# A hybrid attention and delta-rule block on one core: wider products in the pair loop, with halves joined by VectorE, and four smaller moves

## The chip, the cores and the metric

The kernel runs on one core of a Trainium2 chip. The metric is the device time of one execution in microseconds; the times given are those of three executions, and one further execution was profiled. A core has five engines that run side by side and meet at semaphores: TensorE (PE, with its weight loads as PEld), VectorE (DVE), ScalarE (ACT), GpSimd (POOL) and SyncE (SP, which here only starts transfers). Each works through its own instructions in order, so an instruction that waits holds up all that is written behind it on the same engine.

## What is computed

One layer of an encoder block on x (256 rows, 2048 channels), all in 32-bit floats:

```
proj = x @ w_in + b_in                    # columns: aq ak av | dq dk dv dz | db da | ga gb
o_att = sliding-window attention with rotary positions and sinks (aq, ak, av)
q, k, v = silu(causal conv of width 4 (dq, dk, dv)); q, k L2-normalised per head
beta = sigmoid(db); g = -exp(a_log) * softplus(da + dt_bias)
o_dn = gated delta rule over 16 heads of 128, in chunks of 64:
       (I + A) u = beta v, A strictly lower triangular, then a scan over chunks
o_dn = rmsnorm(o_dn) * gain * silu(dz)
mix  = (sigmoid(ga) * (o_att @ w_br_att) + sigmoid(gb) * (o_dn @ w_br_dn)) @ w_out
h    = layernorm(alpha * x + mix)
out  = layernorm(alpha * h + swiglu(h) + sigmoid(h @ w_ple_gate + b) * (p @ w_ple_proj))
```

## The kernel before

**Products in two parts.** A product of 32-bit floats is made of three products of rounded numbers. ScalarE writes `hi`, the rounded copy of a weight tile (L1058), VectorE writes `lo = raw - hi` (L1402), and x lies as `xh` and `xl` in the same way. Both engines' helper is `split`. A quarter is one 128x512 piece of weights; `raw` holds four units of four quarters, loaded on SP's queue, and `hi` and `lo` are rings of eight quarters. The splits run six quarters (`LEAD`) ahead of TensorE, and ScalarE's split number n waits until TensorE has finished with quarter n - 8.

**Two kinds of quarters.** In most stages the weights stream: `rows_quarter` (L586 to L588) makes six products of 512 columns a quarter, with x as the stationary operand. In the pair loop the results are wanted with channels on the partitions, and `cols_quarter` (L574 to L576) has the weights stationary and streams x in 256 columns: for each of two tiles `kk` and two halves `f`, the three products hi\*xh, hi\*xl, lo\*xh go to the same 256 columns of `dense`, twelve products a quarter.

**The pair loop.** The delta rule is done in eight pairs of heads. `mixer_turn(i)` makes the products of pair i in 32 quarters, k = 0 to 31, eight each for dq, dk, dv, dz (s = 0 to 3); turn 0 is unrolled and turns 1 to 7 are a loop. The groups alternate between two pairs of banks of `dense`. ScalarE evicts a group with its bias into `pad` (`pad_in`, at k = 9, 17, 25) or, for dz, into `zb` (`chain_k`, stage 0, in the next turn), and VectorE makes the convolution from `pad`, one tap of one half at each k from 9 on (`conv`). Beside it every turn does one head group of the attention (`att_stage`, `att_k`).

**The chain.** While turn i makes pair i's products, all engines also work on the delta rule of pair i-1, which is one long chain of small steps. Every engine's program goes through the same numbers k, and at k it does the stage `stage_at(k)` of the chain behind its split. That is the whole order of the work: it is written out by hand. Before, `stage_at` gives k for k < 4, nothing at 4, the level matrix 0 (`FIRST`) at 5, and k - 2 from 6 on. The stages which the change and the prediction touch:

- stage 0: TensorE's `kk_qk` (L701, L708) writes k k^T and k q^T into the banks 0 and 1 of `C` (in the trace: chain). It waits for `silk` and `silq` (k and q after silu), and for `am`, the mask addition that VectorE made at k = 29 (L1592). ScalarE evicts `zb` and makes two tanh, for v and for the gate z; VectorE multiplies both (L1650).
- stages 1 to 3: `k_to_rows` (L714), ScalarE's squares (L1159), VectorE's row factors, the product `QKT` (L1656) and `AT` (L1668); ScalarE packs the diagonal blocks of `AT` into `VU` (L1175, L1177).
- the seed: GpSimd sets `VU[2]` to the unit matrix, multiplies the diagonal of `VU[0]` away and subtracts the unit matrix (L520 to L524).
- `FIRST` and stages 5, 7, 9, 11, 13: the inverse of I + A by doubling. VectorE transposes (L1620) and masks (L1622) into `Ym`, TensorE multiplies (`inv_level`, L740), ScalarE evicts (L1214). Level n's product stands at k = 7 + 2n. Stage 4 is an inverse root, eleven small VectorE operations.
- stages 15 to 17: the last doublings, `inv_last_y` (L749) and `inv_last_x` (L758).
- stages 18 to 22: the scan over chunks. L795 and L796 of stage 22 are its last products; ScalarE sums squares (L1203), VectorE adds (L1709).
- stage 23: a second inverse root, and the scaling `tmp` (L1713). Stage 26: transposes (`o_to_cols`, L802). Stage 27: VectorE multiplies with the gate into `odn` (L1717) and raises `on`.

The semaphore `on` is waited for by ScalarE at k = 31. The last pair's chain runs in the gate stage behind the loop, its stages spread over 54 of 64 quarters (`LAST_AT`).

**The start.** x comes in four parts (`x_part`) and is transposed on TensorE with `ident` (L615). The first weights come on ScalarE's queue in two pieces. `keep_busy` (L624) issues filler products before and after the first transposes; `WARM` says how many.

Of the kernel before, what the change touches and what calls it, by code (L numbers as in the profile page):

```python
# [18 lines left out]
F32 = mybir.dt.float32  # L19
F32R = mybir.dt.float32r  # L20
# [6 lines left out]
P = 128  # L27
# [16 lines left out]
WARM = (7, 7)  # L44
# [57 lines left out]
def stage_at(k):  # L102

    return k if k < 4 else k - 2 if k >= 6 else FIRST if k == 5 else None
# [18 lines left out]
def constants():  # L123
# [14 lines left out]
    c[:, C_OFF:C_OFF + 32] = i % 32 != j[:, 0:32]  # L138
# [30 lines left out]
def build(nc, A, out):  # L169
    ctx = ExitStack()  # L170
    with ctx:
# [23 lines left out]
        xh = place("xh", [P, KT, T], F32R)  # L195
        xl = place("xl", [P, KT, T], F32R)
# [157 lines left out]

        def flat2(m):
            return m.rearrange("p a b -> p (a b)")
# [30 lines left out]

        @block.sync
        def _(sp):
# [17 lines left out]

            x_part(0)
            sp.dma_start(ident[:], A["consts"][:, C_IDENT:C_IDENT + P]).then_inc(sem("ident_in"), 16)
# [67 lines left out]
        def _(pool):  # L477
# [38 lines left out]
            def inverse_seed(p):  # L516


                pool.wait_ge(sem("packed"), p + 1)
                pool.tensor_copy(VU[:, 2], four_of(cst[:, C_UNIT:C_UNIT + 32])).then_inc(sem("seed"), 1)  # L520
                pool.tensor_tensor(VU[:, 0], VU[:, 0], four_of(cst[:, C_OFF:C_OFF + 32]),
                                   ALU.mult).then_inc(sem("seed"), 1)
                pool.wait_ge(sem("seed"), 3 * p + 2)
                pool.tensor_tensor(VU[:, 0], VU[:, 0], four_of(cst[:, C_UNIT:C_UNIT + 32]),  # L524
                                   ALU.subtract).then_inc(sem("seed"), 1)

            decay_in(0)
            for p in range(PAIRS):
                inverse_seed(p)
# [33 lines left out]
        def _(pe):  # L563
            def cols_quarter(pos, n, j, bank, mh, ml):
# [3 lines left out]
                for kk in range(2):  # L568
                    k = 2 * j + kk
                    for f in range(2):  # L570
                        wh = hi[:, s, kk * 256 + f * P:kk * 256 + f * P + P]
                        wl = lo[:, s, kk * 256 + f * P:kk * 256 + f * P + P]
                        o = dense[:, bank + f, 0:T]
                        pe.matmul(o, wh, mh[:, k, :], start=(k == 0), stop=False)  # L574
                        pe.matmul(o, wh, ml[:, k, :], start=False, stop=False)  # L575
                        mm = pe.matmul(o, wl, mh[:, k, :], start=False, stop=(k == KT - 1))  # L576
# [120 lines left out]
            def kk_qk(p):  # L697
                pe.wait_ge(sem("silk"), p + 1)
                for x in range(4):
# [31 lines left out]
            def inv_level(p, n):  # L731


                pe.wait_ge(sem("y_out"), nth("y_out", n, p))
                if n:
# [147 lines left out]
            def mixer_turn(i, chain):  # L883

                pos = Pos(4 * U_LOOP, 32, i)
                for k in range(32):
                    s = k // 8
                    if k % 8 == 0:
                        if s == 0 and chain:
                            pe.wait_ge(sem("pad2"), i)  # L890
                        elif s == 1:
                            pe.wait_ge(sem("z_in"), i) if chain else pe.wait_ge(sem("rows_out"), 5)
# [1180 lines left out]
```

## Time and profile before

| | us |
|---|---|
| three executions, median (lowest to highest) | 1932.47 (1932.06 to 1932.5) |
| the profiled execution, its own time | 1932.79 |
| its span in the trace | 1931.0 |
| TensorE busy | 1914.2 |
| VectorE busy | 1269.9 |
| ScalarE busy | 1026.0 |
| GpSimd busy | 37.6 |

The span is the time from the first to the last instruction in the trace; the time of the execution holds 1.8 us around it. Busy time is the time covered by the records of an engine. TensorE's records overlap, since a matmul is recorded until its last result is out, so a stretch in which TensorE is busy throughout may still be one in which it is slower than it could be. In the timeline rows the columns are the start in us from the beginning of the span, the duration in us, the engine, the line and the operation, the output and the inputs, the shape, and the number of instructions merged into the row; in brackets stand the idle time ahead of it and what ended it.

### The profile page before, as it was taken

The page shows a single profiled execution, that of the slowest core. Times are in us where ns is not written, and L with a number is a line of the kernel's source. Part 1 is how long each engine was busy: PE and PEld are TensorE (multiplying, and loading weights), DVE is VectorE, ACT ScalarE, POOL GpSimd, SP SyncE. Part 2 cuts the span into 40 slices and gives each one's busy share as a digit, 9 for nine tenths or more (in the row PEclk, how much of TensorE's full clock was granted, in tenths as well). Part 3 has the DMA queues.
Part 4 walks back from the last instruction along what each step waited for, and adds up shares of the span by engine and source line. Part 5 has one row for each costly group of instructions (what it writes and reads, how often), then busy time and mean ns, then how long its engine had stood idle before and what let it go on. Part 6 is the DMA issues. An engine that isn't in the chain of part 4 may idle for free.

```text
span 1931.0 us, 29904 instructions
## 1 busy us (share of the span) xinstructions
PE 1914.2 (99%) x10563; PEld 1664.6 (86%) x10563; DVE 1269.9 (66%) x2349; ACT 1026.0 (53%) x2068; POOL 37.6 (2%) x79
## 2 busy tenths in 40 slices
PE   9999999999999999999999999999999999999997
PEld 8889999999999888888888788888888888888886
DVE  6657888888888756565665786555555555555555
ACT  4446666666666555455444554545444444444443
POOL 1000000000000000000000000000000000000000
PEclk9999999999999999999999999999999999999999
DMA  8665555455545557566566456555565555666552
GB/s 319 202 159 189 130 143 127 138 119 145 126 137 126 187 170 244 195 202 202 188 236 208 152 198 197 194 193 182 190 196 184 187 194 182 226 201 196 196 194 90
DMA packets 204180, 349.65 MB, mean 181 GB/s; under 512 B 6768, under 2 KB 73024, under 8 KB 203088
## 3 DMA queue, kind: packets, MB, share of 16 engines
q1 hardware_dynamic: 200560, 333.74, 52.6%
q0 software_dynamic: 3264, 14.47, 5.2%
q8 instruction: 44, 0.72, 0.1%
q10 hardware_dynamic: 288, 0.52, 0.1%
q14 instruction: 24, 0.20, 0.0%
HBM read 344.32 MB, written 2.10 MB: 179 GB/s over the span
## 4 chain that ended last, share of the span: by engine, by line
PE 94%; DVE 3%; ACT 1%; issue 1%; DMA 0%; DVEq 0%; SPq 0%; ACTq 0%
PE dense L586 23%; PE dense L588 23%; PE dense L587 23%; PE dense L574 5%; PE dense L575 5%; PE dense L576 5%; PE chain L740 2%; DVE lo L1402 1%; PE chain L822 1%; ACT sE L1238 1%; PE chain L1007 0%; ACT hi L1058 0%; PE chain L749 0%; PE chain L840 0%; PE chain L708 0%
## 5 line engine op out<-in xcount | busy, mean ns | idle before, releaser
L1402 DVE TENSOR_TENSOR lo<-raw,hi 128x512 fp32r<-128x512 f32 x1252 | 849.4, 690 | 525.4 <-ACT hi L1058 522.8
L1058 ACT ACTIVATE hi<-raw 128x512 fp32r<-128x512 f32 x1252 | 774.5, 630 | 628.1 <-PE dense L588 599.0
L586 PE MATMUL dense<-hi,xh 128*128 128x512 f32 x1376 | 539.9, 392 | 1.5 <-DVE xl L1949 1.1
L588 PE MATMUL dense<-lo,xh 128*128 128x512 f32 x1376 | 535.9, 389 | 0.0
L587 PE MATMUL dense<-hi,xl 128*128 128x512 f32 x1376 | 535.5, 389 | 0.0
L586 PEld LDWEIGHTS dense<-hi,xh 128*128 128x128 f32 x1376 | 258.5, 188 | 55.0 <-DVE xl L1949 2.0
L588 PEld LDWEIGHTS dense<-lo,xh 128*128 128x128 f32 x1376 | 258.3, 188 | 54.2
L587 PEld LDWEIGHTS dense<-hi,xl 128*128 128x128 f32 x1376 | 258.6, 188 | 52.4
L574 PE MATMUL dense<-xh,hi 128*128 128x256 f32 x1024 | 303.3, 296 | 0.0
L576 PE MATMUL dense<-xh,lo 128*128 128x256 f32 x1024 | 289.4, 283 | 0.0
L575 PE MATMUL dense<-xl,hi 128*128 128x256 f32 x1024 | 289.2, 282 | 0.0
L574 PEld LDWEIGHTS dense<-xh,hi 128*128 128x128 f32 x1024 | 195.6, 191 | 3.5 <-DVE lo L1402 3.1
L575 PEld LDWEIGHTS dense<-xl,hi 128*128 128x128 f32 x1024 | 195.9, 191 | 0.4
L576 PEld LDWEIGHTS dense<-xh,lo 128*128 128x128 f32 x1024 | 195.4, 191 | 0.0
L586 PE MATMUL dense<-hi,hh 128*128 128x512 f32 x328 | 127.7, 389 | 0.0
L588 PE MATMUL dense<-lo,hh 128*128 128x512 f32 x328 | 127.6, 389 | 0.0
L587 PE MATMUL dense<-hi,hl 128*128 128x512 f32 x328 | 127.6, 389 | 0.0
L586 PE MATMUL dense<-hi,bh 128*128 128x512 f32 x256 | 99.9, 390 | 0.0
L588 PE MATMUL dense<-lo,bh 128*128 128x512 f32 x256 | 99.6, 389 | 0.0
L587 PE MATMUL dense<-hi,bl 128*128 128x512 f32 x256 | 99.6, 389 | 0.0
L588 PEld LDWEIGHTS dense<-lo,hh 128*128 128x128 f32 x328 | 61.6, 188 | 12.9
L587 PEld LDWEIGHTS dense<-hi,hl 128*128 128x128 f32 x328 | 61.6, 188 | 12.8
(318 smaller groups left out, 1531.3 us busy)
## 6 DMA issues: line engine op xcount, KB each, us to landing
raw<-in_w_in_dram SPq DMA_DIRECT2D x115, 1024.0 KB, 5.1
raw<-in_w_ffn_gate_dram SPq DMA_DIRECT2D x44, 1024.0 KB, 5.1
raw<-in_w_ffn_up_dram SPq DMA_DIRECT2D x44, 1024.0 KB, 5.0
raw<-in_w_ffn_down_dram SPq DMA_DIRECT2D x44, 1024.0 KB, 5.0
raw<-in_w_br_att_dram SPq DMA_DIRECT2D x16, 1024.0 KB, 5.0
raw<-in_w_br_dn_dram SPq DMA_DIRECT2D x16, 1024.0 KB, 5.0
raw<-in_w_out_dram SPq DMA_DIRECT2D x16, 1024.0 KB, 5.0
raw<-in_w_ple_gate_dram SPq DMA_DIRECT2D x16, 1024.0 KB, 5.0
```

The lines of the kernel that those rows point to most:

```text
L574: pe.matmul(o, wh, mh[:, k, :], start=(k == 0), stop=False)
L575: pe.matmul(o, wh, ml[:, k, :], start=False, stop=False)
L576: mm = pe.matmul(o, wl, mh[:, k, :], start=False, stop=(k == KT - 1))
L586: pe.matmul(o, ah, hi[:, s, :], start=(k == 0), stop=False)
L587: pe.matmul(o, al, hi[:, s, :], start=False, stop=False)
L588: mm = pe.matmul(o, ah, lo[:, s, :], start=False, stop=(k == nk - 1))
L740: mm = pe.matmul(vu[:, :, x, :], Ym[:, x, :], VU[:, :, x, :], start=True, stop=True)
L822: mm = pe.matmul(o, qT[:, n, 2 * j:2 * j + 2, :].rearrange("p a c -> p (a c)"), kS[:, :, CH * n:CH * n + P], start=True, stop=True)
L1058: act.activation(parts(pos, n)[0], raw[:, slot, off:off + 512], ACT.Copy).then_inc(sem("hi_ready"), 1)
L1238: a = act.activation(m[:, r, :], m[:, r, :], ACT.Exp, bias=sm[:, 2, q:q + 1], scale=ATT_SCALE, accum_out=sm[:, 4, q:q + 1])
L1402: dve.tensor_tensor(wl, raw[:, slot, off:off + 512], wh.bitcast(F32), ALU.subtract).then_inc(sem("lo_ready"), 1)
```

## The change

Five things are done.

1. In `cols_quarter` the products hi\*xh and hi\*xl become one of 512 columns. `xh` and `xl` now lie side by side in one tile `xs`, so that one read gives both. The right half of a bank then holds hi\*xl, and the left one hi\*xh plus lo\*xh. ScalarE evicts the left half as before; VectorE adds the right one, into `pad` at the head of each convolution and into `zb` at stage 4. TensorE waits for these additions (`joined`) before it uses a pair of banks again.
2. The gate's tanh goes from stage 0 to stage 6 and its product from stage 0 to stage 8; the last wait for it is at the squares of the scan.
3. The diagonal is set by one minimum on VectorE at `FIRST`, instead of a multiplication and a subtraction on GpSimd, which keeps the copy of the unit matrix.
4. Stages from 16 on come one quarter later: `stage_at` gives k - 2 up to k = 17, nothing at 18 and k - 3 from 19 on. With that, `kk_qk` waits for `on` of the pair before, since both use bank 1 of `C`.
5. `ident` is the first transfer on SP's queue, the second piece of weights goes from ScalarE's queue to SP's behind the first part of x, and there are 12 and 5 fillers instead of 7 and 7.

The writes of `xh` and `xl` in the other stages (`x_hi`, `x_lo`, `merged_hi`, `merged_lo`, `h1_rows`) are only adapted to the layout and left out here.

```diff
 X_PARTS = (slice(0, 256), slice(256, 512), slice(512, 1024), slice(1024, 2048))
-WARM = (7, 7)
+WARM = (12, 5)
 LAST_AT = {1 + c * 54 // 30: c for c in range(31)}
...
-    return k if k < 4 else k - 2 if k >= 6 else FIRST if k == 5 else None
+    return k if k < 4 else k - 3 if k >= 19 else k - 2 if 6 <= k < 18 else FIRST if k == 5 else None
...
             c[:, C_LAST:C_LAST + 64] = m[:, 0:64]
-    c[:, C_OFF:C_OFF + 32] = i % 32 != j[:, 0:32]
+    c[:, C_OFF:C_OFF + 32] = np.where(i % 32 == j[:, 0:32], -1.0, np.finfo(np.float32).max)
     c[:, C_UNIT:C_UNIT + 32] = i % 32 == j[:, 0:32]
...
         x_at = at[0]
-        xh = place("xh", [P, KT, T], F32R)
-        xl = place("xl", [P, KT, T], F32R)
+        xs = place("xs", [P, KT, 2, T], F32R)
+        xh, xl = xs[:, :, 0, :], xs[:, :, 1, :]
         epsc = place("epsc", [P, 8])
...
+        def first_quarter(engine, k, name):
+            engine.dma_start(raw[:, 0, 512 * k:512 * k + 512], w_in[P * k:P * k + P, AK:AK + 512]).then_inc(sem(name), 16)
...
+            sp.dma_start(ident[:], A["consts"][:, C_IDENT:C_IDENT + P]).then_inc(sem("ident_in"), 16)
             x_part(0)
-            sp.dma_start(ident[:], A["consts"][:, C_IDENT:C_IDENT + P]).then_inc(sem("ident_in"), 16)
+            first_quarter(sp, 1, "second_in")
             x_part(1)
...
-            def inverse_seed(p):
-                pool.wait_ge(sem("packed"), p + 1)
+            def unit_blocks(p):
+                if p:
+                    pool.wait_ge(sem("u_last"), p)
                 pool.tensor_copy(VU[:, 2], four_of(cst[:, C_UNIT:C_UNIT + 32])).then_inc(sem("seed"), 1)
-                pool.tensor_tensor(VU[:, 0], VU[:, 0], four_of(cst[:, C_OFF:C_OFF + 32]),
-                                   ALU.mult).then_inc(sem("seed"), 1)
-                pool.wait_ge(sem("seed"), 3 * p + 2)
-                pool.tensor_tensor(VU[:, 0], VU[:, 0], four_of(cst[:, C_UNIT:C_UNIT + 32]),
-                                   ALU.subtract).then_inc(sem("seed"), 1)
...
             for p in range(PAIRS):
-                inverse_seed(p)
+                unit_blocks(p)
                 if p + 1 < PAIRS:
...
         def _(pe):
-            def cols_quarter(pos, n, j, bank, mh, ml):
+            def cols_quarter(pos, n, j, bank):
...
                         wl = lo[:, s, kk * 256 + f * P:kk * 256 + f * P + P]
-                        o = dense[:, bank + f, 0:T]
-                        pe.matmul(o, wh, mh[:, k, :], start=(k == 0), stop=False)
-                        pe.matmul(o, wh, ml[:, k, :], start=False, stop=False)
-                        mm = pe.matmul(o, wl, mh[:, k, :], start=False, stop=(k == KT - 1))
+                        pe.matmul(dense[:, bank + f, :], wh, xs[:, k].rearrange("p u n -> p (u n)"),
+                                  start=(k == 0), stop=False)
+                        mm = pe.matmul(dense[:, bank + f, 0:T], wl, xh[:, k, :], start=False, stop=(k == KT - 1))
                 mm.then_inc(sem("quarter_done"), 1)
...
                 pe.wait_ge(sem("silk"), p + 1)
+                if not isinstance(p, int) or p:
+                    pe.wait_ge(sem("on"), p)
                 for x in range(4):
...
                 pe.wait_ge(sem("y_out"), nth("y_out", n, p))
+                if n == 0:
+                    pe.wait_ge(sem("seed"), p + 1)
                 if n:
...
                         if s == 0 and chain:
-                            pe.wait_ge(sem("pad2"), i)
+                            pe.wait_ge(sem("joined"), 4 * i - 1)
                         elif s == 1:
-                            pe.wait_ge(sem("z_in"), i) if chain else pe.wait_ge(sem("rows_out"), 5)
+                            pe.wait_ge(sem("joined"), 4 * i) if chain else pe.wait_ge(sem("rows_out"), 5)
                         elif s == 2:
-                            pe.wait_ge(sem("pad0"), i + 1)
+                            pe.wait_ge(sem("joined"), 4 * i + 1)
                         elif s == 3:
-                            pe.wait_ge(sem("pad1"), i + 1)
-                    cols_quarter(pos, k, k % 8, 2 * ((s + 1) % 2), xh, xl)
+                            pe.wait_ge(sem("joined"), 4 * i + 2)
+                    cols_quarter(pos, k, k % 8, 2 * ((s + 1) % 2))
                     if chain:
...
                 if n == 0:
-                    pe.wait_ge(sem("pad2"), PAIRS)
+                    pe.wait_ge(sem("joined"), 4 * PAIRS - 1)
                 elif n == 16:
-                    pe.wait_ge(sem("z_in"), PAIRS)
+                    pe.wait_ge(sem("joined"), 4 * PAIRS)
                 elif n % 16 == 0:
...
         def _(act):
-            for k, name in enumerate(("first_in", "second_in")):
-                act.dma_start(raw[:, 0, 512 * k:512 * k + 512], w_in[P * k:P * k + P, AK:AK + 512]).then_inc(sem(name), 16)
+            first_quarter(act, 0, "first_in")
...
                                        bias=bcol[:, ds(16 * s + f + 2 * i, 1)])
-                r.then_inc(sem(f"pad{s}"), 1)
+                r.then_inc(sem("evicted"), 1)
...
                                            bias=bcol[:, ds(48 + f + 2 * p, 1)])
-                    r.then_inc(sem("z_in"), 1)
+                    r.then_inc(sem("evicted"), 1)
                     act.wait_ge(sem("conv2"), 2 * p + 2)
                     act.activation(flat(QKT[:]), flat(cv[:]), ACT.Tanh, scale=0.5).then_inc(sem("tanh"), 1)
-                    act.wait_ge(sem("z_in"), p + 1)
-                    act.activation(flat(bv[:]), flat(zb[:]), ACT.Tanh, scale=0.5).then_inc(sem("tanh"), 1)
                 elif k == 1:
...
                     act.wait_ge(sem("v_rows"), p + 1)
-                    act.wait_ge(sem("silz"), p + 1)
                     act.activation(flat(bv[:]), C[:, 3, :], ACT.Copy, scale=0.5).then_inc(sem("v_copied"), 1)
...
                                    scale=RMS_EPS * P).then_inc(sem("q_eps"), 1)
+                elif k == 6:
+                    act.wait_ge(sem("joined"), 4 * p + 4)
+                    act.activation(flat(tmp[:]), flat(zb[:]), ACT.Tanh, scale=0.5).then_inc(sem("tanh"), 1)
                 elif k in (18, 21):
...
                     act.wait_ge(sem("o_prod"), nth("o_prod", c, p))
+                    act.wait_ge(sem("silz"), p + 1)
                     for h in range(2):
...
                 if n % 8 == 0:
-                    dve.wait_ge(sem(f"pad{s}"), i + 1)
+                    dve.wait_ge(sem("evicted"), 4 * i + s + 1)
+                    b0 = 2 * ((s + 1) % 2)
+                    dve.tensor_tensor(pad[:, :, 3:T + 3], pad[:, :, 3:T + 3], dense[:, b0:b0 + 2, T:2 * T],
+                                      ALU.add).then_inc(sem("joined"), 1)
+                    dve.wait_ge(sem("joined"), 4 * i + s + 1)
                 tap = cw[:, j, ds(16 * s + f + 2 * i, 1)]
...
-                    for n, (th, dst, name) in enumerate(((QKT, cv, "silv"), (bv, zb, "silz"))):
-                        dve.wait_ge(sem("tanh"), nth("tanh", 2 + n, p))
-                        dve.scalar_tensor_tensor(flat(dst[:]), flat(th[:]), 1.0, flat(dst[:]), ALU.add,
-                                                 ALU.mult).then_inc(sem(name), 1)
+                    dve.wait_ge(sem("tanh"), nth("tanh", 2, p))
+                    dve.scalar_tensor_tensor(flat(cv[:]), flat(QKT[:]), 1.0, flat(cv[:]), ALU.add,
+                                             ALU.mult).then_inc(sem("silv"), 1)
                 elif k == 1:
...
                                       each(kdecs[:, 0, ds(2 * p, 2)], 2), ALU.mult).then_inc(sem("kdec"), 1)
+                elif k == 8:
+                    dve.wait_ge(sem("tanh"), nth("tanh", 3, p))
+                    dve.scalar_tensor_tensor(flat(zb[:]), flat(tmp[:]), 1.0, flat(zb[:]), ALU.add,
+                                             ALU.mult).then_inc(sem("silz"), 1)
                 elif k == 4:
+                    dve.wait_ge(sem("evicted"), 4 * p + 4)
+                    dve.tensor_tensor(zb[:], zb[:], dense[:, 0:2, T:2 * T], ALU.add).then_inc(sem("joined"), 1)
                     inverse_root("length", row[:, 1, :], row[:, 4, :], p)
...
                 elif k == FIRST:
-                    dve.wait_ge(sem("seed"), 3 * p + 3)
+                    dve.wait_ge(sem("packed"), p + 1)
+                    dve.tensor_tensor(VU[:, 0], VU[:, 0], four_of(cst[:, C_OFF:C_OFF + 32]),
+                                      ALU.min).then_inc(sem("off_unit"), 1)
+                    dve.wait_ge(sem("off_unit"), p + 1)
                     level_matrix(p, 0, flat(VU[:, 0]))
```

## Rows read from the trace of the kernel before

**Rows 1.** The page's busy times (share of the span) and its granted clock

```profile
PE 1914.2 (99%) x10563; PEld 1664.6 (86%) x10563; DVE 1269.9 (66%) x2349; ACT 1026.0 (53%) x2068; POOL 37.6 (2%) x79
...
PEclk9999999999999999999999999999999999999999
```

**Rows 2.** Busy time by engine in 65 us of the loop, with its columns

```profile
core 0: us, PE busy (x) PEld busy (x) DVE busy (x) ACT busy (x) POOL busy (x), PEclk, DMA share, GB/s
390.00:455.00 65.00, 64.73 (x540) 63.50 (x538) 55.12 (x140) 41.94 (x122) 2.29 (x5) 1.00 0.53 133
```

**Rows 3.** TensorE's timeline at the end of quarter 0 and `kk_qk`

```profile
441.78 0.28 PE L576 MATMUL dense<-xh,lo 128*128 128x256 f32 x1
...
441.90 1.06 PE L701 MATMUL chain<-ck 128*128 128x128 f32 x8
```

**Rows 4.** TensorE's timeline in a later stage, first and last of 14 products

```profile
1299.69 0.39 PE L586 MATMUL dense<-hi,xh 128*128 128x512 f32 x1
...
1302.63 0.39 PE L587 MATMUL dense<-hi,xl 128*128 128x512 f32 x1
```

**Rows 5.** TensorE's timeline of the turn from 441.90

```profile
455.05 1.13 PE L740 MATMUL chain<-VU,Ym 128*128 128x96 f32 x8
...
459.57 1.13 PE L740 MATMUL chain<-VU,Ym 128*128 128x96 f32 x8
...
479.53 0.28 PE L576 MATMUL dense<-xh,lo 128*128 128x256 f32 x1
...
480.00 1.10 PE L749 MATMUL chain<-Tm,AT 128*128 128x64 f32 x8 [0.19 <-DVE Tm L1643]
...
493.87 0.39 PE L795 MATMUL chain<-S,qd 128*128 128x128 f32 x2
...
506.71 1.06 PE L701 MATMUL chain<-ck 128*128 128x128 f32 x8
```

**Rows 6.** GpSimd's and VectorE's timeline of the same turn, levels 0 and 1

```profile
452.29 0.46 POOL L524 TENSOR_TENSOR VU<-VU,cst 128x128 f32<-128x128 f32 x1
...
453.96 0.30 DVE L1620 STREAM_TRANSPOSE Vt<-VU 128x128 f32<-128x128 f32 x1
...
454.30 0.69 DVE L1622 TENSOR_TENSOR Ym<-Vt,cst 128x512 f32<-128x512 f32 x1
...
458.74 0.69 DVE L1622 TENSOR_TENSOR Ym<-Vt,cst 128x512 f32<-128x512 f32 x1
```

**Rows 7.** VectorE's timeline of the same turn, two prices

```profile
446.38 0.68 DVE L1656 TENSOR_TENSOR QKT<-chain,Em 128x512 f32<-128x512 f32 x1
...
460.56 0.42 DVE L1685 TENSOR_TENSOR qd<-cq,qd 128x256 f32<-128x256 f32 x1
```

**Rows 8.** VectorE's timeline of the same turn, its end

```profile
495.83 0.48 DVE L1580 SCALAR_TENSOR_TENSOR ck<-pad,cw,ck 128x256 f32<-128x256 f32 x1
...
496.24 0.68 DVE L1402 TENSOR_TENSOR lo<-raw,hi 128x512 fp32r<-128x512 f32 x1
...
504.55 0.74 DVE L1717 SCALAR_TENSOR_TENSOR odn<-chain,ghalf,zb 128x512 f32 x1
...
505.21 0.68 DVE L1592 TENSOR_TENSOR Em<-G,cst 128x512 f32<-128x512 f32 x1
```

**Rows 9.** ScalarE's timeline of the same turn, the eviction of v's group

```profile
496.51 0.84 ACT L1124 ACTIVATE pad<-dense,bcol 128x256 f32<-128x256 f32 x2 [0.40 <-PE dense L576]
```

**Rows 10.** Timeline of the first 10 us, TensorE and VectorE

```profile
1.22 3.36 PE L624 MATMUL chain<-kS 128*128 128x128 f32 x14 [1.22 <-POOL kS L479]
...
5.87 1.12 PE L615 MATMUL chain<-ident,xrow 128*128 128x128 f32 x4 [1.29 <-DMA ident<-in_consts_dram]
...
6.78 3.19 PE L624 MATMUL chain<-kS 128*128 128x128 f32 x14
...
7.65 0.69 DVE L1418 TENSOR_TENSOR xl<-chain,xh 128x512 fp32r<-128x512 f32 x1 [1.87 <-ACT xh L1065]
...
9.62 0.67 PE L586 MATMUL dense<-hi,xh 128*128 128x512 f32 x1
```

More of the change, by code:

```diff
@@ L353, in flat, with two @@
             return m.rearrange("p a b -> p (a b)")
+        def two(m):
+            return m.rearrange("p (k n) -> p k n", k=2)
         def flat2(m):
@@ L1064, in x_hi @@
                 act.wait_ge(sem("x_cols"), b + 1)
-                act.activation(flat(xh[:, 2 * b:2 * b + 2, :]), C[:, b % 4, :], ACT.Copy).then_inc(sem("x_hi"), 1)
+                act.activation(xh[:, 2 * b:2 * b + 2, :], two(C[:, b % 4, :]), ACT.Copy).then_inc(sem("x_hi"), 1)
             split(Pos(0), 0)
@@ L1282, in merged_hi @@
                 act.wait_ge(sem("m_cols"), b + 1)
-                act.activation(flat(xh[:, 2 * b:2 * b + 2, :]), C[:, b % 4, :], ACT.Copy,
+                act.activation(xh[:, 2 * b:2 * b + 2, :], two(C[:, b % 4, :]), ACT.Copy,
                                scale=0.5).then_inc(sem("m_hi"), 1)
@@ L1417, in x_lo @@
                 dve.wait_ge(sem("x_hi"), b + 1)
-                dve.tensor_tensor(flat(xl[:, 2 * b:2 * b + 2, :]), C[:, b % 4, :],
-                                  flat(xh[:, 2 * b:2 * b + 2, :]).bitcast(F32), ALU.subtract).then_inc(sem("x_lo"), 1)
+                dve.tensor_tensor(xl[:, 2 * b:2 * b + 2, :], two(C[:, b % 4, :]),
+                                  xh[:, 2 * b:2 * b + 2, :].bitcast(F32), ALU.subtract).then_inc(sem("x_lo"), 1)
             split(Pos(0), 0)
@@ L1844, in merged_lo @@
                 dve.wait_ge(sem("m_hi"), b + 1)
-                dve.scalar_tensor_tensor(flat(xl[:, 2 * b:2 * b + 2, :]), C[:, b % 4, :], 0.5,
-                                         flat(xh[:, 2 * b:2 * b + 2, :]).bitcast(F32), ALU.mult,
+                dve.scalar_tensor_tensor(xl[:, 2 * b:2 * b + 2, :], two(C[:, b % 4, :]), 0.5,
+                                         xh[:, 2 * b:2 * b + 2, :].bitcast(F32), ALU.mult,
                                          ALU.subtract).then_inc(sem("m_lo"), 1)
@@ L1948, in h1_lo @@
                 dve.wait_ge(sem("h1_whole"), b + 1)
-                dve.tensor_tensor(flat(xl[:, 2 * b:2 * b + 2, :]), flat(whole[:, b % 2]), flat(xh[:, 2 * b:2 * b + 2, :]).bitcast(F32),
+                dve.tensor_tensor(xl[:, 2 * b:2 * b + 2, :], whole[:, b % 2], xh[:, 2 * b:2 * b + 2, :].bitcast(F32),
                                   ALU.subtract).then_inc(sem("h1_lo"), 1)
```

## The prediction

> **What bounds the kernel now.** I read the page first. TensorE is busy for nearly the whole span and VectorE for two thirds of it [rows 1]. That says TensorE is the bound on average, but VectorE's share is a mean over stages, so the second view is the busy time of one turn of the pair loop: in 65 us VectorE is busy 55.12 [rows 2]. In the loop VectorE has under 10 us to spare, and the loop is where the change adds to it.
>
> The third view is the timeline of TensorE over one turn. The start of one matmul to the start of the next is what a matmul costs in a stream, not the 0.28 us of its record: the 128x256 products start every 0.12 us [rows 3], the 128x512 products of the later stages every 2.94 / 13 = 0.226 us [rows 4]. One turn runs from one `kk_qk` to the next, 506.71 - 441.90 = 64.81 us [rows 3, 5]. The waits in it are small: `inv_last_y` at 480.00 started 0.47 us behind the last loop product, where 0.12 is the rule, and the level product at 459.57 some 0.2 us late, just behind the `Ym` that VectorE ended at 458.74 + 0.69 = 459.43 [rows 5, 6]. The one before it is as close: `Ym` is complete at 454.30 + 0.69 = 454.99 and the product starts at 455.05. So TensorE sets the turn, with VectorE right behind it in two places. That is what decides this change.
>
> **The products.** A quarter of the loop is 12 products of 256 columns, 12 x 0.12 = 1.44 us. After the change it is four pairs of one 512 and one 256, 4 x (0.226 + 0.12) = 1.385 us: the columns are the same, and one start in three is saved. That is 0.055 us a quarter, 1.8 us in the 32 quarters of a turn, 14 us in eight turns, if TensorE sets them.
> Of the 0.12 us of a product, 256 columns at the upper level of the clock (2.4 GHz; granted 1.00 in this stretch [rows 2]) explain 0.107; the remaining 0.013 is what a saved start is worth. The Trainium skill, page "TensorE: Matmul & The Clock Gate", section "Back-to-back issue gap", puts that remainder at about 2.5 ns. An estimate by it would be 1024 x 2.5 ns = 2.6 us for the loop where the rows give 14. Both shapes have rows here and they disagree with the page, so the rows are used.
>
> **The additions on VectorE.** Each group's right half is added after ScalarE's eviction: three joins into `pad` and one into `zb`, 128x512 with one operand in PSUM. The nearest row is the product of `chain` and `Em`, 0.68 us, of which about 0.61 shows when another instruction follows and 0.73 when VectorE waits for its own result, as the convolution now does [rows 7]. Bounds 0.6 and 0.75 each. The minimum on the diagonal moves two operations of GpSimd, the last at 452.29 + 0.46 = 452.75 and thus hidden before VectorE's first transpose at 453.96 [rows 6], onto VectorE in front of that transpose. A 128x256 tensor operation takes 0.42 us [rows 7]; half the columns and the wait for its own result make 0.33 (bounds 0.25 and 0.45). The gate's product (0.6 us) leaves step 0 for step 10, so it changes no sum. Together VectorE gets 3 x 0.73 + 0.61 + 0.33 = 3.1 us more per turn, in a turn that should become shorter.
>
> **Where this comes to lie: three places.**
> First, the end of a pair. Stages from 16 on come one quarter later, so the last scan product (L795) stands in quarter 25 and `on`, the write of `odn`, at VectorE's step 30; and `kk_qk` of the next turn now waits for `on`, behind which all further products are queued on TensorE. Before: L795 at 493.87, `kk_qk` at 506.71, 12.84 us later; `on` at 504.55 + 0.74 = 505.29, 11.42 after L795 [rows 5, 8]. TensorE now has one quarter less in between and seven quarters shorter by 0.055: 12.84 - 1.44 - 0.39 = 11.0. VectorE from L795 to `on`: behind the sum of squares (L1709) came a convolution step and a split before the root of step 23; these, 495.83 to 496.84, 1.0 us in all, now lie before the wait for the squares; the mask addition (L1592), a convolution step and a split come ahead of `on`, 0.6 + 0.4 + 0.6; and the join of v's group stands in between, 0.73, after ScalarE's eviction, which in program order follows the squares and takes 0.84 [rows 8, 9], so VectorE waits about 0.5 there. 11.42 - 1.0 + 1.6 + 0.73 + 0.5 = 13.25. TensorE waits 13.25 - 11.0 = 2.2 us in each turn, a part of it perhaps already at `o_to_cols`.
> Second, the first level. From `kk_qk` to the first complete `Ym` it was 454.99 - 441.90 = 13.09; the way goes over ScalarE's squares, the rows of `AT` and the packing into `VU`, and nothing that the change takes out lies on it: the gate's tanh and product leave ScalarE and VectorE before them, but both then wait for the rows of k. With the minimum it is 13.42, where TensorE would be there after 13.15 - 7 x 0.055 = 12.77: 0.65 us of waiting.
> Third, the second level. Between the two `Ym` VectorE had no gap, 458.74 - 454.30 = 4.44; the join of `zb` comes in between, 5.05. TensorE had 4.52, of which 0.2 was waiting, and would need 4.2: 0.85 us more.
> What is gained in return: the 0.35 us before `inv_last_y`, which is now a quarter later, and the 0.2 counted above. Further levels have 1 to 2 us of slack, which these delays use up; 0 to 0.4 us more, I take 0.1.
>
> **The sum.** `kk_qk` to the second level 13.42 + 5.05 + 0.1 for the reactions = 18.6. From there to L795: 493.87 - 459.57 = 34.30, plus a quarter 1.44, less 16 x 0.055 = 0.9, less 0.35, plus 0.1: 34.6. Then 13.3 to the next `kk_qk`. 66.5 us a turn instead of 64.8, that is 1.7 longer. Of the seven such intervals six are in the loop: +10.2. The last ends behind one more 512-column quarter of the gate stage (6 x 0.226 = 1.4, so 66.2 before): +0.3. Turn 0 has no chain and gains its 1.8. The chain of the last pair lies spread over the gate stage, where nothing waits; its additions cost nothing there.
> The start: seven fillers ran from 1.22 to 4.6, 0.48 us each, TensorE then stood until `ident` landed at 5.87, and seven more ended only at 9.6, later than the operands that they cover (`xl` is complete at 7.65 + 0.69 = 8.34). All of it went at half the later rate, as at the lower level of the clock, though the page's line of the granted clock is too coarse to show it [rows 1]; the first L586, at 9.62, still has 0.67 us where 0.39 is usual [rows 4, 10]. With `ident` first it lands half a microsecond earlier, x's first part as much later, near 6, and twelve fillers end between 1.22 + 12 x 0.24 = 4.1 and 1.22 + 12 x 0.48 = 7.0: hardly a pause. I take it that the rate rises before the transposes, at 6.1; from their start to `xl` it was 8.34 - 5.87 = 2.5, four transposes at the full rate save 0.45, and the first quarter starts near 8.2 and is not slow itself: 1.6 us less. Bounds: 0, if the rate stays low (then 12 and 5 fillers take what 7, the pause and 7 took), and 2. The second piece of weights, moved from ScalarE's queue to SP's behind `x_part(0)`, starts about half a microsecond later, and so do the transfers queued behind it on SP; `x_part(0)` aside they are wanted only after the first columns' eviction, past 7 us, and are covered.
> The other edits (the layout of `xs`, the strided writes) change no shape: nothing.
> Sum: +10.2 + 0.3 - 1.8 - 1.6 = +7.1. On the profiled execution's 1932.8 that is 1939.9, and on the median, 0.3 below it, 1939.6 us.
>
> **Rivals.** (A) The other side: TensorE keeps setting the turns, since VectorE's added work falls into its 10 us of idle time. Against it stand the two `Ym` that came within 0.15 us of their products. For it: the shares of the page, and that VectorE still waits for TensorE elsewhere. Its place is L740 and `kk_qk`; it decides if `on` is there 11.0 us after L795. Then 14 + 7 x 0.55 + 1.6 = 19.5 us less: 1913.
> (B) Only the wait for `on` shows, and the two levels keep up, because the front of the chain is ahead after the wait. Then 19.5 less, 6 x 2.2 + 0.8 more: 1927.
> (C) VectorE's lateness spreads to all levels, 0.6 to 1 us a turn more than I take: 1944 to 1947.
> (D) The change doesn't do what it says: a weight load, recorded with 0.19 us, does not fit behind the 256-column product that now follows a long one, and a pair costs 0.36 us as before. Then 23 quarters of a turn that TensorE sets lose 0.055 each, 1.3 a turn, and turn 0 gains nothing: 1950. Against it: loads now start every 0.12 us already.
>
> **How the numbers follow.** My forecast 0.66, A 0.09, B 0.11, C 0.08, D 0.06. A measurement of this kernel can tell about 0.2% from no change, 3.9 us. Faster: A and most of B, 0.18. Same: the rest of B and the low end of the forecast (joins at 0.6, minimum at 0.25, no wait for the eviction: a turn of 65.7, 1935), 0.10. Slower: 0.72. The range goes from 1927 (half of B in) to 1945 (the forecast with 0.4 more a turn, and part of C); left out are A, the rest of B, D and most of C.
>
> **What would show it.** After: the product L740 of level 0 and of level 1 right behind `Ym`, both with an idle time; `kk_qk` right behind the end of the `odn` product with 1 to 2 us of idle time on TensorE; from L795 to the next `kk_qk` some 13.3 us; starts of the pair of products 0.346 us apart; a turn of about 66.5. A turn under 64 proves me wrong, and so does a `kk_qk` that starts without a wait. In the stages behind the loop nothing should have moved. At the start the first L586 should be near 8.2.

## The result, and the profile after

The changed kernel takes 1951.8 us (median of 4, 1951.66 to 1952.75) against 1932.49 in the same session, 1.0100 times as long (95% interval 1.0088 to 1.0112): 19.3 us slower, where I had forecast 7.1. The direction and the three places were right; the size was not, and the time lies outside the range.

The page of the changed kernel, its busy times:

```profile
PE 1914.1 (98%) x9545; PEld 1607.2 (82%) x9545; DVE 1293.0 (66%) x2389; ACT 1023.7 (52%) x2068; POOL 32.8 (2%) x63
```

Against [rows 1] TensorE is as busy as before although it has a thousand matmuls less, and VectorE has 23 us more. The span grew by 19. Where, the starts of `kk_qk` tell: 182.35 and 637.65 for the first and the last one before, 181.01 and 656.52 after. The seven intervals between them grew by 20.2 us: six of some 64.8 to some 67.9 (+3.06 each on average), the one into the gate stage from 66.1 to 68.0. All before them gained 1.3, all behind them lost 0.1.

TensorE's timeline of one turn of the changed kernel, 452.79 to 520.63. L706 is `kk_qk`, L747 `inv_level`, L829 the attention's scores, L802 the last scan product, L809 `o_to_cols`; it answers to [rows 5]:

```profile
452.79 1.16 PE L706 MATMUL chain<-ck 128*128 128x128 f32 x8 [1.42 <-DVE odn L1736]
...
466.31 0.91 PE L747 MATMUL chain<-VU,Ym 128*128 128x96 f32 x6 [0.28 <-DVE Ym L1633]
...
471.41 1.13 PE L747 MATMUL chain<-VU,Ym 128*128 128x96 f32 x8 [0.32 <-DVE Ym L1633]
...
476.09 1.02 PE L747 MATMUL chain<-VU,Ym 128*128 128x96 f32 x8
...
477.46 0.92 PE L829 MATMUL chain<-kS,qT 128*128 128x256 f32 x3 [0.35 <-DVE sE L1744]
...
507.19 0.38 PE L802 MATMUL chain<-S,qd 128*128 128x128 f32 x2
...
514.31 0.65 PE L809 MATMUL chain<-ident,tmp 128*128 128x128 f32 x4 [0.41 <-DVE tmp L1732]
...
520.63 1.16 PE L706 MATMUL chain<-ck 128*128 128x128 f32 x8 [1.50 <-DVE odn L1736]
```

Every wait in it is for VectorE. `kk_qk` is held up for `odn`, both first levels for `Ym`, the scores for `sE`. VectorE's timeline at these places (L1695 is the minimum, L1690 and L1580 are joins, L1686 the gate's product); it answers to [rows 6, 8]:

```profile
464.89 0.28 DVE L1695 TENSOR_TENSOR VU<-VU,cst 128x128 f32<-128x128 f32 x1
...
465.56 0.69 DVE L1633 TENSOR_TENSOR Ym<-Vt,cst 128x512 f32<-128x512 f32 x1
...
466.77 0.68 DVE L1690 TENSOR_TENSOR zb<-zb,dense 128x512 f32<-128x512 f32 x1
...
470.58 0.69 DVE L1633 TENSOR_TENSOR Ym<-Vt,cst 128x512 f32<-128x512 f32 x1
...
476.00 0.69 DVE L1686 SCALAR_TENSOR_TENSOR zb<-tmp,zb 128x512 f32<-128x512 f32 x1
...
476.99 0.41 DVE L1744 TENSOR_SCALAR sE<-chain 128x256 f32<-128x256 f32 x1
...
509.67 0.69 DVE L1580 TENSOR_TENSOR pad<-pad,dense 128x512 f32<-128x512 f32 x1 [0.57 <-ACT pad L1130]
...
519.83 0.74 DVE L1736 SCALAR_TENSOR_TENSOR odn<-chain,ghalf,zb 128x512 f32 x1
```

The turn, laid against the working of the prediction:

| us | before | forecast | after |
|---|---|---|---|
| `kk_qk` to the level 1 product | 17.67 | 18.6 | 18.62 |
| level 1 product to the last scan product | 34.30 | 34.6 | 35.78 |
| last scan product to the next `kk_qk` | 12.84 | 13.3 | 13.44 |
| the turn | 64.81 | 66.5 | 67.84 |

### The profile page after: what moved, and what is told of

The parts are those of the page before. It is cut to its first block, busy times and chain, and to the rows that moved or that the text cites. A ratio compares the mean times of both kernels' runs of the same rounds, so it can differ in the third digit from the quotient of the medians.

```text
span 1950.0 us, 27935 instructions
## 1 busy us (share of the span) xinstructions
PE 1914.1 (98%) x9545; PEld 1607.2 (82%) x9545; DVE 1293.0 (66%) x2389; ACT 1023.7 (52%) x2068; POOL 32.8 (2%) x63
## 4 chain that ended last, share of the span: by engine, by line
PE 84%; DVE 8%; issue 4%; ACT 2%; DMA 1%; DVEq 1%; ACTq 0%; POOL 0%; SPq 0%; POOLq 0%
PE dense L589 22%; PE dense L591 22%; PE dense L590 22%; PE dense L577 6%; PE dense L579 3%; DVE lo L1409 2%; DMA raw<-in_w_in_dram 1%; PE chain L747 1%; DVE pad L1580 1%; ACT hi L1064 1%; PE chain L1014 0%; PE chain L839 0%; PE chain L706 0%; PE chain L847 0%; PE chain L829 0%
## 5 line engine op out<-in xcount | busy, mean ns | idle before, releaser
L1064 ACT ACTIVATE hi<-raw 128x512 fp32r<-128x512 f32 x1252 | 773.0, 630 | 618.4 <-PE dense L591 595.4
L589 PE MATMUL dense<-hi,xs 128*128 128x512 f32 x1376 | 539.8, 392 | 1.7 <-DVE xs L1968 1.1
L591 PE MATMUL dense<-lo,xs 128*128 128x512 f32 x1376 | 535.9, 389 | 0.0
L590 PE MATMUL dense<-hi,xs 128*128 128x512 f32 x1376 | 535.5, 389 | 0.0
L577 PE MATMUL dense<-xs,hi 128*128 128x512 f32 x1024 | 380.3, 410 | 1.0
L589 PEld LDWEIGHTS dense<-hi,xs 128*128 128x128 f32 x1376 | 258.4, 188 | 55.5 <-DVE xs L1968 2.0
L591 PEld LDWEIGHTS dense<-lo,xs 128*128 128x128 f32 x1376 | 258.3, 188 | 54.2
L590 PEld LDWEIGHTS dense<-hi,xs 128*128 128x128 f32 x1376 | 258.5, 188 | 52.4
L579 PE MATMUL dense<-xs,lo 128*128 128x256 f32 x1024 | 286.2, 280 | 0.0
L577 PEld LDWEIGHTS dense<-xs,hi 128*128 128x128 f32 x1024 | 192.6, 188 | 44.3 <-issue 5.2
L579 PEld LDWEIGHTS dense<-xs,lo 128*128 128x128 f32 x1024 | 193.6, 189 | 0.4
L589 PE MATMUL dense<-hi,hh 128*128 128x512 f32 x328 | 127.7, 389 | 0.0
L589 PE MATMUL dense<-hi,bh 128*128 128x512 f32 x256 | 99.9, 390 | 0.0
L589 PEld LDWEIGHTS dense<-hi,hh 128*128 128x128 f32 x328 | 61.6, 188 | 12.5
L589 PEld LDWEIGHTS dense<-hi,bh 128*128 128x128 f32 x256 | 48.1, 188 | 9.9
```

The lines of the kernel that those rows point to most:

```text
L577: pe.matmul(dense[:, bank + f, :], wh, xs[:, k].rearrange("p u n -> p (u n)"), start=(k == 0), stop=False)
L579: mm = pe.matmul(dense[:, bank + f, 0:T], wl, xh[:, k, :], start=False, stop=(k == KT - 1))
L589: pe.matmul(o, ah, hi[:, s, :], start=(k == 0), stop=False)
L590: pe.matmul(o, al, hi[:, s, :], start=False, stop=False)
L591: mm = pe.matmul(o, ah, lo[:, s, :], start=False, stop=(k == nk - 1))
L1064: act.activation(parts(pos, n)[0], raw[:, slot, off:off + 512], ACT.Copy).then_inc(sem("hi_ready"), 1)
```

## The experiments

Fourteen kernels, one change each where that could be. The names say what was done; "turn" is the usual interval between two `kk_qk`, 64.81 us before and 67.85 in the changed kernel.

**The stages moved back.** The only edit:

```diff
-    return k if k < 4 else k - 3 if k >= 19 else k - 2 if 6 <= k < 18 else FIRST if k == 5 else None
+    return k if k < 4 else k - 2 if k >= 6 else FIRST if k == 5 else None
```

> The changed kernel with the old stage numbers (all stages from 6 on at k - 2), nothing else. Theory (the end of the chain is too late for kk_qk, since odn is made at step 30 and behind a join): TensorE's wait at kk_qk and the one at o_to_cols, 1.4 to 1.9 and 0.4 us a turn, go; inv_last_y waits for Tm again, about 1 us, because the join of k's group now lies ahead of it. A turn near 66.5 us instead of 67.85, the kernel at 1941 to 1945. Rival (VectorE's total work sets the turn, wherever it lies): the turn stays at 67.8 and the kernel at 1951 to 1952.

1945.02 us, a turn of 66.80, the slow end of what the theory said. The waits for `odn` and `tmp` are gone, and in their place stands the one that the move was to remove, now for a `Tm` behind the join of k's group (TensorE's timeline):

```profile
488.53 1.10 PE L756 MATMUL chain<-Tm,AT 128*128 128x64 f32 x8 [0.99 <-DVE Tm L1654]
```

So the move costs 1.05 us a turn net. VectorE's work is the same in both, so the rival falls.

**The products put back**, the rest as changed (what waited for `joined` waits for the eviction again):

```diff
-                        pe.matmul(dense[:, bank + f, :], wh, xs[:, k].rearrange("p u n -> p (u n)"),
-                                  start=(k == 0), stop=False)
-                        mm = pe.matmul(dense[:, bank + f, 0:T], wl, xh[:, k, :], start=False, stop=(k == KT - 1))
+                        o = dense[:, bank + f, 0:T]
+                        pe.matmul(o, wh, xh[:, k, :], start=(k == 0), stop=False)
+                        pe.matmul(o, wh, xl[:, k, :], start=False, stop=False)
+                        mm = pe.matmul(o, wl, xh[:, k, :], start=False, stop=(k == KT - 1))
...
-                    dve.tensor_tensor(pad[:, :, 3:T + 3], pad[:, :, 3:T + 3], dense[:, b0:b0 + 2, T:2 * T],
-                                      ALU.add).then_inc(sem("joined"), 1)
...
-                    dve.tensor_tensor(zb[:], zb[:], dense[:, 0:2, T:2 * T], ALU.add).then_inc(sem("joined"), 1)
```

> The changed kernel with the twelve 256-column products a quarter and without the four joins; stages, gate, minimum and start as changed. Theory (the joins on VectorE's path cost more than the wider products save): the level 1 product comes 0.6 us earlier after level 0, odn 1.3 us earlier after the last scan product, the sE wait shrinks: a turn of 65.8 us, 1936 to 1940. Rival (the late stages and the wait for on cost the time by themselves): a turn of 67 us or more, 1946 to 1952.

1942.53 us, a turn of 66.46: between the two. Wider products and joins together cost 1.4 us a turn here. But even without them the turn is 1.65 longer than before, above all since `kk_qk` still waits for `odn`:

```profile
514.26 0.94 PE L707 MATMUL chain<-ck 128*128 128x128 f32 x6 [1.31 <-DVE odn L1731]
```

**Products, joins and gate alone**, on the kernel before (the old stages, seed and start).

> The kernel before with only the 512-column products, the joins and the later gate; stages, GpSimd's seed and the start as before. Theory: waits of TensorE at level 1 (0.9 us), at the attention's second scores (0.5) and at inv_last_y (about 1), none at kk_qk: a turn of 65.8 to 66.3 us against 64.8, 1938 to 1943. Rival (the products and joins cost nothing by themselves, the loss is in the shift): at most 1933.

1943.56 us, a turn of 66.50, just above the theory's upper end: +1.68. TensorE's waits for level 0, level 1, `sE` (0.5 us) and `Tm` (1.2 us) were there, none at `kk_qk`.

**The minimum back on GpSimd.**

> The changed kernel with the diagonal made by GpSimd again. Theory (the minimum lies on the path between kk_qk and the first level): kk_qk to the level 0 product falls by 0.3 us, the turn by the same, the kernel by 2 us to 1949.5. Rival (something else bounds this stretch, such as the splits): no change, 1951.5 to 1952.

1949.02 us, a turn of 67.52: 0.33 less, and the rival falls. The three parts now add up: 1.68 (products, joins, gate) + 1.05 (stages) + 0.33 (minimum) = 3.06, and 67.85 - 64.81 = 3.04 was to be explained.

**The wait for `on` behind the k-k products.** The wait moves from the head of `kk_qk` to in front of the k-q products.

> The changed kernel with the wait for on behind the four k-k products of kk_qk (which use another bank) and ahead of the k-q products only. First theory: all that follows on TensorE comes earlier by the 0.9 to 1.0 us of these products, a turn of 66.9 us, 1945. Rival, now the likelier: ScalarE itself waits for on at k = 31 and then needs 3.8 us of its own work (Em, a split, two evictions, a tanh, a split) before the squares, and had only 0.3 us of idle time ahead of them, so the turn falls by 0.3 us to 67.5 and the kernel to 1949.7.

A turn of 67.53, 0.3 less, 1951.09 us as the median of two times that lie 2.6 us apart, so the turn decides. The rival holds: behind the wait at TensorE stands one of ScalarE for the same `odn`, 6 us long, as its timeline in the changed kernel shows:

```profile
520.70 0.40 ACT L1146 ACTIVATE Em<-Em,gneg 128x128 f32<-128x128 f32 x1 [6.14 <-DVE odn L1736]
```

**The gate's product at stage 12**, behind `sE` instead of ahead of it.

> The changed kernel with the gate's product on VectorE at stage 12 (k = 14) instead of stage 8 (k = 10), where it stands ahead of sE. Theory: the 0.5 us that TensorE waits for sE at the attention's second scores goes, the level 3 product comes 5.12 - 0.5 us after level 2, the turn falls by 0.4 to 0.5 us, the kernel to 1948 to 1949. Rival (the next level on VectorE is just as late and takes the time back): turn unchanged at 67.85, 1951.5.

1950.34 us, a turn of 67.70: 0.15 less, and neither forecast. The wait for `sE` went, but one for the attention's `sE` product (L1767) came further on, at its transposes. Taking one piece off a stretch in which VectorE has no gap moves the wait on.

**The order of the products**, 512, 512, 256, 256 for the two halves f.

> The changed kernel with the products of a tile in the order 512, 512, 256, 256 instead of 512, 256, 512, 256. A pair now takes 0.353 us where the single prices, 0.226 and 0.12, make 0.346. Theory (the extra lies in the change from short to long, where the long one's start to the next is 0.24): two pairs take 0.700 instead of 0.707, a quarter 0.014 less, the turn 0.2 us less since only half of it is set by TensorE: 1950. Rival (no dependence on the order): a quarter as before, 1951.8.

1951.93 us, a turn of 67.88: no gain, although the four quarters from 3 to 6, with the transposes of v ahead of them, did take 6.03 us, between the 6.09 of the changed kernel and the 6.19 of before. In a turn that VectorE sets, that is worth nothing.

**The start undone.**

> The changed kernel with 7 and 7 fillers, ident second and both first pieces of weights on ScalarE's queue. The changed start begins the first quarter 1.9 us earlier, but TensorE then stands 1.4 us for dbT. Theory (dbT is bound through VectorE's splits to the landing of the weights of quarter 20, which comes at 34.3 to 34.6 us whatever the start): the kernel is slower by only 0.5 to 0.7 us, 1952.4. Rival (the gain is kept): slower by 1.9 us, 1953.7.

1952.32 us. The 0.5 more that the theory says can't be told from nothing (the changed kernel's own times reach from 1951.66 to 1952.75), but the 1.9 more of the rival is not there, and the traces show why. The first L589 of the changed kernel stood at 7.72, where the kernel before had 9.62 and this run has 9.17. Over all sixteen traces the first quarter starts at 7.98 to 9.77 with the old start and at 7.35 to 8.59 with the new one, so a single pair of traces does not fix the gain to better than about 1 us. Then, from the timelines of ScalarE, VectorE and TensorE of the changed kernel (L1064 is `split`, here of quarters 20 and 21):

```profile
34.64 1.15 ACT L1064 ACTIVATE hi<-raw 128x512 fp32r<-128x512 f32 x2 [1.40 <-DMA raw<-in_w_in_dram]
...
41.87 0.47 DVE L1473 TENSOR_SCALAR dbT<-chain,dbcol 32x256 f32<-32x256 f32 x1
...
42.39 0.63 PE L672 MATMUL chain<-cst,dbT 64*128 64x32 f32 x4 [1.40 <-DVE dbT L1473]
```

In the kernel before these three stood at 34.33, 41.56 and 42.97, and TensorE did not wait: `dbT` was complete at 42.03, 0.9 us ahead of its use. The start has moved by 1.9, the landing has not, and most of the difference is the wait. VectorE makes `dbT` behind splits 20 and 21, and in all sixteen traces, with either start, ScalarE's split 20 starts between 34.2 and 35.1, when its weights land.

**The joins left out**, on the kernel of products and gate: the right halves, hi\*xl of the pair loop, are missing in the result.

> The kernel before with the 512-column products and the later gate, but without the four joins: the right halves (the products hi*xl of the pair loop) are computed and left out of the result. Theory (a pair of products costs 0.353 us, so the wider products save 0.85 us a turn and not 1.8, and all else of the loss is the joins): a turn of 64.0 us against 64.8 before and 66.5 with the joins, the kernel at 1925 to 1927. Rival (VectorE sets the turn even without the joins): a turn of 64.7 or more, 1931.

1926.20 us, 0.9968 of before (0.9956 to 0.9981), a turn of 64.16. The wider products, with the gate at stage 8, gain 0.65 us a turn, and the joins alone cost 66.50 - 64.16 = 2.34. On VectorE they take 3 x 0.85 + 0.60 = 3.15 us (from 509.67 the next instruction starts at 510.52, since it waits for the result). Three quarters of what the joins add on VectorE lengthens the turn.

**The gate alone**, on the kernel before.

> The kernel before with only the gate's tanh at stage 6 and its product at stage 12. Theory (the front of the chain goes over ScalarE's squares and VectorE's rows, which wait for the transposed k either way, so taking the gate out of stage 0 gains nothing there): the turn stays at 64.8 us within 0.1, 1931.5 to 1932.8. Rival (the gate was on the path to level 0): a turn of 64.2, 1928.

1932.37 us (0.9998, 0.9989 to 1.0008), a turn of 64.82: nothing, as expected. The product stands at stage 12 here, though, and at stage 8 in the changed kernel; at stage 8 it was run only with the wider products, where TensorE did not wait for `sE` once the joins were out.

**The changed start with VectorE's splits 20 and 21 behind `dbT`**, on the kernel before:

```diff
-            for n in range(8, 16 + LEAD):
+            for n in range(8, 20):
...
                               ALU.add).then_inc(sem("dbda_cols"), 1)
+            for n in range(20, 16 + LEAD):
+                split(Pos(0), n)
```

> The kernel before with the changed start (ident first, 12 and 5 fillers) and VectorE's splits 20 and 21 put behind dbT, so that dbT no longer waits for the weights of quarter 20. Theory: the 1.9 to 2.0 us that the changed start gains are kept, 1930.2 to 1930.7. Rival (something else in the first 45 us takes the place of that wait): 1931.5 to 1932.

1931.22 us (0.9994, 0.9984 to 1.0003), a span of 1929.2 against 1931.0. In the trace the loop starts 1.7 us earlier and `dbT` is no longer waited for; of the times themselves the gain is not told from none.

**With `Tm` ahead of the first tap at k = 17.**

> As start_and_order, and at k = 17 VectorE turns the rows (Tm) ahead of the convolution's first tap of the next group, which waits for ScalarE's eviction. Theory: TensorE's wait of 0.35 us ahead of inv_last_y goes in each of seven turns: a turn of 64.4 to 64.5, 1927.8 to 1928.3. Rival (the transpose waits for the level product anyway): as start_and_order.

1928.97 us, 0.9982 (0.9972 to 0.9992), a turn of 64.52. This is the fastest complete kernel of the study, 3.5 us below before. The changed start and the two reorderings do it without a product touched.

**Both products wide**, on the kernel without joins: lo times both halves too, unused on the right.

> joins_left_out with the third product 512 columns wide as well (lo times both halves of x; its right half and that of the first product are left out of the result). It measures the price of a pair of which both are wide. Theory (0.24 is what a 512-column product with weights as the stationary operand costs in this stage, against 0.226 in the late stages): a pair takes 0.48 us. Rival (the change from a short to a long product costs the extra 0.007 to 0.014): a pair takes 0.453 us, as in the late stages.

2027.29 us, a turn of 76.63, which is nearly the price of the columns; the rival holds. TensorE's timeline:

```profile
442.26 0.40 PE L580 MATMUL dense<-xs,hi 128*128 128x512 f32 x1
442.50 0.40 PE L582 MATMUL dense<-xs,lo 128*128 128x512 f32 x1
442.73 0.39 PE L580 MATMUL dense<-xs,hi 128*128 128x512 f32 x1
```

A wide product costs 0.23 here. In the changed kernel, the same view:

```profile
459.06 0.40 PE L577 MATMUL dense<-xs,hi 128*128 128x512 f32 x1
459.30 0.28 PE L579 MATMUL dense<-xs,lo 128*128 128x256 f32 x1
459.41 0.40 PE L577 MATMUL dense<-xs,hi 128*128 128x512 f32 x1
```

0.24 and 0.11, a pair in 0.353.

**The joins on GpSimd.** ScalarE copies the right half to a tile of its own and GpSimd adds it; the changed start and the two reorderings are in.

> The kernel before with the 512-column products, the later gate, the start and the two reorderings of rows_first, and the joins taken off VectorE: ScalarE copies the right half to a tile of its own (0.6 us each) and GpSimd adds it. From GpSimd's 0.46 us for 128x128 I estimate 1.8 us for an addition. Theory (the loss is VectorE's time, not the additions as such): most of the 0.65 us a turn of joins_left_out is kept, a turn of 64.2 to 65.0 us, 1925 to 1930. Rival (VectorE's first tap waits for GpSimd at k = 9 and k = 17, and the level products with it): a turn of 66 us or more, 1938.

1937.08 us (1.0023, 1.0013 to 1.0033), a turn of 65.75: between the forecasts. With `Tm` first a complete kernel has 64.5, so the joins still cost more than the products gain. The addition took GpSimd only 1.09 us into `pad`, and 1.29 into `zb`. What is lost lies at the front of the chain: the product of level 0 stands 14.2 us behind `kk_qk`, where it is 13.1 without joins, and TensorE waits there for `Ym`; the rest of the turn is within 0.3 us of that of the run with `Tm` first.

The joins have not left VectorE either. From the timelines of GpSimd and VectorE:

```profile
500.65 1.09 POOL L541 TENSOR_TENSOR pad<-pad,right 128x512 f32<-128x512 f32 x1 [16.63 <-ACT right L1144]
500.76 1.00 DVE L1633 SCALAR_TENSOR_TENSOR row<-row 128x4 f32<-128x4 f32 x1
```

Elsewhere this small operation of the second inverse root takes 0.16 us; the one that meets GpSimd's addition ends only with it. In all seven turns the same three VectorE instructions are recorded long, each beside an addition: this one with 0.84 us more, the product of v (L1670, 1.37 instead of 0.69) beside the addition into `zb`, and a product of q (L1709, 1.31 instead of 0.42) beside the one of q's group. That is 2.4 us a turn of VectorE's time, and for the fourth addition VectorE's first tap waits 1.27 us. In the loop these are the only kinds of VectorE instructions that are over 0.1 us longer than the longest in the run with `Tm` first. At the front two of these (the small operation, ahead of the mask addition, and the product of v) and ScalarE's copy of `zb`'s right half (0.5 us ahead of the tanh) come together; what each costs there was not separated. What a copy placed later, or additions placed in VectorE's gaps, would give was not tried.

## Why the prediction was right in direction and wrong in size

**The end of the pair** was right. Last scan product to the end of `odn`: 13.25 forecast, 13.38 measured, and to `kk_qk` 13.3 and 13.44; VectorE waited 0.57 for the eviction (0.5 forecast), and the join took 0.85 with the wait for its result (0.73 forecast); TensorE waited 0.57 at `o_to_cols` and 1.67 at `kk_qk` (1.78 behind the last product less the usual 0.11), 2.24 together, 2.2 forecast.

**The first two levels** were right. The minimum and its wait took 0.32 (464.89 to the transpose at 465.21), the undoing gave 0.33; from one `Ym` to the next it was 5.02 (5.05 forecast); the product of level 1 stands where it was forecast. One wait was not forecast and cost nothing: behind level 0 TensorE stands 0.3 us for the join of `zb` (467.58), and then waits for `Ym` at level 1 all the same.

**The price of a pair** was the first step that failed: "four pairs of one 512 and one 256, 4 x (0.226 + 0.12) = 1.385 us". Both prices came from streams of one length. In the changed kernel a pair took 0.353, the saving was 0.007 instead of 0.014 a pair, 0.9 us a turn instead of 1.8. Of the 16 quarters between level 1 and the last scan product that is 16 x 0.028 = 0.45 us a turn.

The Trainium skill's rule (page "TensorE: Matmul & The Clock Gate", section "Back-to-back issue gap") makes an estimated 0.3 us a turn of the saved starts; the trace, with 0.9, does not agree with that either.

**"Further levels have 1 to 2 us of slack, which these delays use up; 0 to 0.4 us more, I take 0.1"** was the second. I had laid the additions ahead of levels 0 and 1 against the slack behind them, but not the gate's product, which I had moved to step 10 with the words that "it changes no sum". It stands ahead of `sE` there, and TensorE waits for `sE` at L829, 0.5 us. With smaller waits behind it (the attention's transposes, the state) it makes 0.7. The experiment with stage 12 shows that the place alone was not it: VectorE has no gap of note from the splits at 463.68 to k = 17. So the stretch from level 1 to the last scan product took 35.78 instead of 34.6, and with 0.2 at the end that is the 1.3 us a turn that were missing, some 8 us in six turns.

**The last interval** cost 1.9 instead of 0.3. That `on` sets it, and not the quarter more that TensorE has to do in it, was right: it was 68.0, like the others. The forecast was short there by what it was short in every turn, and 0.25 more. Together: 6 x 1.35 + 1.6 here + 1.0 at the start + 1.0 in turn 0 = 11.7 of the 12 us that were missing.

**The start** was right up to the first quarter (7.72, forecast 8.2; part of it luck, since this place scatters by about 1 us) and wrong behind it: I checked that transfers up to 12 us were covered, not those at 34. Of 1.6 us 0.6 was left at the end of the first stage, and turn 0 gained 0.8 instead of 1.8, by the price of the pair.

Of the rivals A and B fell with the waits; D was half true, in that the pair cost more than its parts but less than three products; C, the spreading of VectorE's lateness, came nearest. VectorE's part of what was missing, 0.7 us in the middle and 0.14 at the end, lies within its 0.6 to 1 us a turn; but it came at the attention's scores and not at the levels, where from the third on TensorE waited for nothing, and the dearer pair came on top of it.

That VectorE's path was what had no room, is shown by taking work off it: the joins left out give back 2.34 us, the minimum 0.33, and moving stages without changing any work 1.05. gpsimd_joins does not add to that. It is 0.75 us a turn faster than the joins on VectorE, but it also has `Tm` first, and in products_and_gate_only TensorE waited 1.2 us a turn for that `Tm` behind a join; and GpSimd's additions held VectorE up. The joins on VectorE with `Tm` first were not run.

## What to carry to other kernels

Where an in-order engine has a long stretch without a gap, every operation added to it lengthens the loop by most of its time, whatever the engine's mean share (55 of 65 us busy here, and 2.34 of 3.15 us came through). Lay each added or moved operation against the waits of all that comes behind it up to the next real gap, not against the nearest consumer. Take a price for a mix of shapes from a mix, and before counting an earlier start as a gain, look for the first transfer that lands at its own time. And when an operation goes to another engine, look whether the first engine's instructions beside it have kept their length: here they had not.

## What the runs showed that I had not expected

The mixed pair has two prices. From `v_to_rows` to `q_to_rows`, with 16 pairs in between, the turns of the kernel without joins took either 5.98 or 6.09 us: a pair in 0.346, the sum of its single prices, or in 0.353, and nothing in between. Pair by pair, the cheap stretches alternate between 0.350 and 0.344, the dear ones run 0.350, 0.350, 0.360. The changed kernel had 6.09 in all seven turns, the products and gate alone 5.98 in five and 6.1 in two, and the order 512, 512, 256, 256 had 6.01 to 6.03 in all. What decides between them no run here told.

GpSimd added 128x512 in 1.09 us, where four times its record for 128x128, 0.46, had made me expect 1.8.
